# Gate and up products of three feed-forwards: the high weights meet both halves of the activations in one 512-column matmul

## The reference

```python
def swiglu(h, w_gate_up, w_down):
    gu = jnp.einsum("bsd,df->bsf", h, w_gate_up)
    g, u = jnp.split(gu, 2, axis=-1)
    return jnp.einsum("bsf,fd->bsd", jax.nn.silu(g) * u, w_down)

x = x + rmsnorm(swiglu(rmsnorm(x, g_pre), w_gate_up, w_down), g_post)        # first block
x = x + 0.5 * swiglu_2(rms_norm(x, norm_ffn1), ffn1_w1, ffn1_w3, ffn1_w2)    # second block, start
x = x + 0.5 * swiglu_2(rms_norm(x, norm_ffn2), ffn2_w1, ffn2_w3, ffn2_w2)    # second block, end
```

## Time and profile before

| | |
|---|---|
| median of 3 runs | 1049.44 us (1048.48 to 1049.68) |
| profiled execution, first to last instruction (span) | 1046.5 us |
| mean granted TensorE clock | 0.994 |
| TensorE matmul / weight load busy | 1022.3 / 1007.0 us |
| VectorE / ScalarE / GpSimd busy | 651.0 / 493.6 / 115.3 us |
| matmul records | 8282 |

### The profile page before, as it was taken

One profiled execution on the slowest core, in us unless ns is written; L12 is line 12 of the kernel. 1 busy time (PEld: TensorE's weight loads), 2 busy tenths in 40 slices (PEclk: granted clock), 3 DMA queues, 4 the chain that ended last, 5 costly groups with the idle time before them and its releaser, 6 DMA issues.

```text
span 1046.5 us, 19409 instructions
## 1 busy us (share of the span) xinstructions
PE 1022.3 (98%) x8282; PEld 1007.0 (96%) x8282; DVE 651.0 (62%) x616; ACT 493.6 (47%) x625; POOL 115.3 (11%) x91
## 2 busy tenths in 40 slices
PE   8999999998999999989999999999999999999997
PEld 7998999998999999979999999999999999999996
DVE  6655767958655555595555557775684475555554
ACT  5443445645433434554343434655755564343433
POOL 5000000566000000450000002000030020000000
PEclk9999999999999999999999999999999999999999
DMA  8653364453545565545646464633444345555531
GB/s 277 206 163 120 121 242 162 134 188 122 200 162 200 164 198 168 182 137 198 197 164 200 160 200 162 200 123 122 162 161 147 116 161 168 194 171 190 183 138 41
DMA packets 138107, 175.39 MB, mean 168 GB/s; under 512 B 3940, under 2 KB 122950, under 8 KB 137926
## 3 DMA queue, kind: packets, MB, share of 16 engines
q1 hardware_dynamic: 136006, 171.24, 49.7%
q10 hardware_dynamic: 2048, 3.38, 0.9%
HBM read 173.56 MB, written 1.05 MB: 167 GB/s over the span
## 4 chain that ended last, share of the span: by engine, by line
PE 88%; DVE 7%; issue 2%; ACT 1%; POOL 1%; DMA 1%; SPq 0%; DVEq 0%; ACTq 0%; POOLq 0%
PE bank L373 27%; PE bank L374 27%; PE bank L375 27%; DVE act_lo L1437 3%; DVE w_lo L1424 1%; PE bank L457 1%; DVE x_T L1539 1%; PE bank L821 1%; PE bank L842 1%; DMA stage<-in_w_in 1%; ACT w_hi L899 1%; PE bank L460 0%; PE bank L600 0%; DVE w_lo L1561 0%; PE bank L616 0%
## 5 line engine op out<-in xcount | busy, mean ns | idle before, releaser
L373 PE MATMUL bank<-act_hi,w_hi 128*128 128x256 f32 x1648 | 471.8, 286 | 12.7 <-DVE act_lo L1437 9.2
L374 PE MATMUL bank<-act_lo,w_hi 128*128 128x256 f32 x1648 | 467.5, 284 | 0.0
L375 PE MATMUL bank<-act_hi,w_lo 128*128 128x256 f32 x1648 | 467.4, 284 | 0.0
L373 PEld LDWEIGHTS bank<-act_hi,w_hi 128*128 128x128 f32 x1648 | 317.3, 193 | 18.1 <-DVE act_lo L1437 7.6
L374 PEld LDWEIGHTS bank<-act_lo,w_hi 128*128 128x128 f32 x1648 | 317.6, 193 | 0.1
L375 PEld LDWEIGHTS bank<-act_hi,w_lo 128*128 128x128 f32 x1648 | 317.4, 193 | 0.0
L1430 DVE TENSOR_TENSOR w_lo<-stage,w_hi 128x2048 fp32r<-128x2048 f32 x81 | 185.6, 2292 | 141.3 <-ACT w_hi L906 141.3
L1424 DVE TENSOR_TENSOR w_lo<-stage,w_hi 128x2048 fp32r<-128x2048 f32 x79 | 183.9, 2333 | 90.1 <-ACT w_hi L899 89.7
L899 ACT ACTIVATE w_hi<-stage 128x2048 fp32r<-128x2048 f32 x79 | 150.7, 1910 | 72.9 <-PE bank L375 71.0
L906 ACT ACTIVATE w_hi<-stage 128x2048 fp32r<-128x2048 f32 x81 | 154.0, 1902 | 54.8 <-PE bank L375 54.8
L373 PE MATMUL bank<-ffn_hi,w_hi 128*128 128x256 f32 x480 | 135.9, 283 | 0.0
(11 more groups left out here) (300 smaller groups left out, 1233.9 us busy)
## 6 DMA issues: line engine op xcount, KB each, us to landing
stage<-in_ffn_w SPq DMA_DIRECT2D x66, 1024.0 KB, 5.1
stage<-in_w_in SPq DMA_DIRECT2D x33, 1024.0 KB, 5.2
stage<-in_w_gate_up SPq DMA_DIRECT2D x22, 1024.0 KB, 5.1
stage<-in_w_down SPq DMA_DIRECT2D x11, 1024.0 KB, 4.8
stage<-in_w_out SPq DMA_DIRECT2D x8, 1024.0 KB, 4.9
stage<-in_mem_w_kv SPq DMA_DIRECT2D x8, 1024.0 KB, 5.3
stage<-in_w_branch SPq DMA_DIRECT2D x4, 1024.0 KB, 5.4
stage<-in_mem_w_q SPq DMA_DIRECT2D x4, 1024.0 KB, 4.9
```

Source lines behind the costliest of these rows:

```text
L373: pe.matmul(dst, w, x, start=first, stop=False, skip_group_check=not group)
L374: pe.matmul(dst, w, lo_x, start=False, stop=False, skip_group_check=not group)
L375: return pe.matmul(dst, lo_w, x, start=False, stop=last, skip_group_check=not group)
```

## The change

`act_hi` and `act_lo` become the two halves of one tile, so that for each k the 256 columns of the high part and the 256 of the low part are neighbours. In gate and up chunks, a step loads the high weights once and streams all 512 columns into a whole bank (first half high·high, second half high·low); the low weights' matmul of 256 columns adds to the second half. A chunk so takes two banks (one for each m): gate chunks have banks 2 and 3, up chunks banks 0 and 1, and gate 1 no longer has a bank of its own kind. 32 matmuls a chunk instead of 48, the same number of columns.

VectorE reads a chunk with a reduction that adds the two halves, 1024 elements into 512. rs is applied in operations of their own: to g after its reduction, and to the silu result; the up sum is multiplied with that. The square sum ahead of a feed-forward goes to bank ACC. Gate chunks wait for `gate_read`, up chunks for `up_read`. Outside the gate and up chunks of the feed-forwards no matmul changes.

```diff
-        act_hi = sb("act_hi", [P, KD, T], F32R)
-        act_lo = sb("act_lo", [P, KD, T], F32R)
+        act_both = sb("act_both", [P, KD, 2, T], F32R)
+        act_hi, act_lo = act_both[:, :, 0, :], act_both[:, :, 1, :]
...
+        up_banks, gate_banks = (ctx.enter_context(nc.psum_tensor(n, [P, 2, 512], F32)) for n in ("up_banks", "gate_banks"))
+        bank = [x[:, i, :] for x in (up_banks, gate_banks) for i in range(2)]
...
+        gate_halves, up_halves = (x[:, :, :].rearrange("p m (s t) -> p m t s", s=2) for x in (gate_banks, up_banks))
...
+            def halves_product(banks, place, ready=None, base=0):
...
+                def step(m, k):
+                    ms = slice(m * P, m * P + P)
+                    pe.matmul(banks[:, m, :], wh[:, k, ms], act_both[:, k, :, :].rearrange("p s t -> p (s t)"),
+                              start=k == 0, stop=False, skip_group_check=True)
+                    return pe.matmul(banks[:, m, T:2 * T], wl[:, k, ms], act_both[:, k, 0, :],
+                                     start=False, stop=k == KD - 1, skip_group_check=True)
...
+            def feed_forward(f, prep, norm, banks_before, extra=None):
+                base, n = FFN[f], f * PAIRS
+                pe.wait_ge(lo_done, base + 1)
+                aux(A_BEFORE_FFN[f])
+                pe.wait_ge(std_done, norm)
+                halves_product(gate_banks, base % RING, act_lo_done, 8 * prep)
+                sums(norm, ACC)
+                pe.wait_ge(lo_done, base + 2)
+                for c in banks_before:
+                    wait_read(pe, c)
+                halves_product(up_banks, (base + 1) % RING)
...
                 def body(t, first):
                     c = base + 2 + t * 3
                     pe.wait_ge(lo_done, c + 1)
+                    pe.wait_ge(gate_read, t + (n + 1))
+                    halves_product(gate_banks, s[0])
                     if first:
-
-                        aux(A_BEFORE_FFN[f])
-                    else:
-                        pe.wait_ge(up_free, t * 2 + (free + 1))
-                    up_product(pair[AUX if first else UP], s[0], act_hi, act_lo)
+                        pe.wait_ge(std_done, norm + 1)
...
                     ffn_chunk(c + 1, f, t, first, s[1])
                     pe.wait_ge(lo_done, c + 3)
-                    pe.wait_ge(up_free, t * 2 + (free + 2))
-                    up_product(pair[UP + 1], s[2], act_hi, act_lo)
+                    pe.wait_ge(up_read, t + (n + 1))
+                    halves_product(up_banks, s[2])
...
-                def gate_part(t, i, src=pair[UP]):
+                def gate_part(t, i):
+                    n = f * PAIRS + i + 1
                     dve.wait_ge(used, t * 3 + (base + (2 + 3 * (i - 1) if i else 0) + 1))
-                    dve.tensor_tensor(g_s, src, over(rs), ALU.mult).then_inc(up_free, 1)
+                    dve.tensor_reduce(g_s, gate_halves, AX, ALU.add).then_inc(gate_read, 1)
+                    dve.wait_ge(gate_read, t + n)
+                    dve.tensor_tensor(g_s, g_s, over(rs), ALU.mult).then_inc(gate_scaled, 1)
+
+                def silu_part(t, i):
+                    dve.wait_ge(silu_done, t + (f * PAIRS + i + 1))
+                    dve.tensor_tensor(silu, silu, over(rs), ALU.mult).then_inc(silu_scaled, 1)
...
-                    dve.tensor_tensor(u_s, pair[UP + 1], over(rs), ALU.mult).then_inc(up_free, 1)
-                    dve.wait_ge(up_free, t * 2 + (u0 + 2 * i + 2))
-                    dve.wait_ge(silu_done, t + n)
+                    dve.tensor_reduce(u_s, up_halves, AX, ALU.add).then_inc(up_read, 1)
+                    dve.wait_ge(up_read, t + n)
+                    dve.wait_ge(silu_scaled, t + n)
                     dve.tensor_tensor(h_T, u_s, silu, ALU.mult).then_inc(h_done, 1)
...
+                with dve.Fori(0, PAIRS - 2) as t:
                     lo_in_loop(t, base + 4)
-                    gate_part(t, 1, src)
+                    gate_part(t, 1)
                     lo_in_loop(t, base + 5)
+                    silu_part(t, 1)
                     lo_in_loop(t, base + 6)
                     up_part(t, 1, base + 4)
```

More of the change, by code:

```diff
@@ L40 @@
 FFN_CHUNKS = 3 * PAIRS
[L43 to L51, removed]
+BANK, BEFORE, FREED, AFTER_FFN = {}, {}, {}, {}
 BY_ACT = {V, V + 1, *range(OUT1, OUT1 + 4), *range(MEMK, MEMK + 4), *MEMV, DQ, DQ + 1, RV, RV + 1, DV, DV + 1,
@@ L71 @@
 through_banks(range(MEMQ, MEMQ + 4))
-through_banks(ffn_ups(FFN[2]))
-UP_FFN = [FREED[b] - 1 for b in FFN]
+AFTER_FFN[MEMV[0]] = AFTER_FFN[MEMV[1]] = 0
+AFTER_FFN[MEMV[3]] = AFTER_FFN[DQ] = 1
 def made(n):
@@ L426, in sums @@
                     pe.wait_ge(std_done, n)
-                pe.matmul(bank[SUM][:, 0:T], ones, sq_acc[:, 0, :], start=True, stop=True).then_inc(sum_done, 1)
+                pe.matmul(bank[to][:, 0:T], ones, sq_acc[:, 0, :], start=True, stop=True).then_inc(sum_done, 1)
             def sums_by_token(n):
@@ L487, in ffn_chunk @@
                      k_done if f == 0 and first == "first" else None)
[L489 to L493, removed]
+            def halves_product(banks, place, ready=None, base=0):
+                wh = w_hi[:, place, :].rearrange("p (k n) -> p k n", k=KD)
+                wl = w_lo[:, place, :].rearrange("p (k n) -> p k n", k=KD)
+                def step(m, k):
[4 more added lines that the diff above has]
+                                     start=False, stop=k == KD - 1, skip_group_check=True)
+                if ready is None:
+                    for m in range(2):
+                        for k in range(KD):
+                            mm = step(m, k)
+                else:
+                    for k in range(KD):
+                        pe.wait_ge(ready, base + k + 1)
+                        for m in range(2):
+                            mm = step(m, k)
+                mm.then_inc(used, 1)
+            def feed_forward(f, prep, norm, banks_before, extra=None):
[9 more added lines that the diff above has]
+                halves_product(up_banks, (base + 1) % RING)
                 s = [(base + 2 + j) % RING for j in range(3)]
@@ L1161, in _ @@
             hi(34)
-            deviation(3)
+            deviation(3, ACC)
             warm(ACT.Silu)
@@ L1183, in _ @@
             hi(70)
-            deviation(5)
+            deviation(5, ACC)
             warm(ACT.Silu)
@@ L1384, in _ @@
             hi(130)
-            deviation(8)
+            deviation(8, ACC)
             warm(ACT.Silu)
```

49 lines of the change are left out of this document (27 added, 22 removed).

## The result

| | before | after |
|---|---|---|
| median of 7 runs | 1049.74 us | 1052.95 us |
| ratio | | 1.0031 (95% interval 1.0020 to 1.0042) |
| span of the profiled execution | 1046.5 us | 1050.3 us |
| matmul records | 8282 | 7226 |

The change makes the kernel 0.31% slower, and the interval leaves no room for a gain. The forecast was 1038 us, faster. The profile before is of the fastest of its seven executions (1048.48 us), the one after of an execution 0.84 us under its median, so the spans differ by 3.8 us and the medians by 3.2.

A forecast was written before the change was run, and what follows sets the result against it. TensorE alone was taken to bound the feed-forwards. Savings of 4.45 us in the second and third and 3.0 in the first took 11.9 off 1046.5; with 2.94 for the median, 1037.5, say 1038 us; range 1033 to 1060.

The forecast's parts named there:

- the period: Three chunks (gate, up, down) inside a feed-forward on TensorE; forecast to go from 17.28 to 16.51 us.
- VectorE's longer ring: VectorE's in-order round with ScalarE, one up read to the next; forecast to grow from 13.82 to 16.30 us.
- TensorE, gate and up chunks: Gate and up matmuls: wide one 216 ns, narrow one 120, a step 336; each chunk 0.38 us less.
- rival B: Gate and up chunks: 13.3 ns stay with each matmul, wide one 226.6 ns; total 1046 us; chance 0.22.
- handovers: From the last down chunk of the first or second feed-forward to the next one's first up chunk; forecast change 0.
- rival C: Gate and up chunks: cost is by the column, wide matmul 237.3 ns; total 1054.5 us, slower; chance 0.12.
- Rival D: VectorE's two reductions: the split read is slow, 2.29 us each, VectorE becomes the bound; total 1100 us; chance 0.22.
- Start: Each feed-forward's start: gate 1 must wait for gate 0's reduction; 2.1 us later in the first, 1.07 in the others.
- End: Last chunks of a feed-forward: VectorE has less time, so the last down chunk waits; 0.62 us net loss each.
- D10: Last of a feed-forward's down chunks, numbered 0 to 10; forecast to start 17.9 us after the end of up 9.
- G10 and U10: Last gate and up chunks of a feed-forward, numbered 0 to 10; forecast to gain 0.77 us together.
- the prediction's own sums: Per feed-forward: start wait, less the saving of 16 chunks (15 in the first), plus 0.6 us at the end.

The follow-up runs named there:

- the uniform runs: A kernel of nothing but matmuls, 48 of one form back to back, each with its own weight load; in fp32r 120.0 ns for 256 columns, 227.5 for 512.
- the first run with GpSimd: Changed kernel with wide and narrow matmuls grouped, gate 0 read early, a low part moved, and silu's product with rs on GpSimd; 1045.02 us, ratio 0.9945.

## Why the prediction was wrong

*What bounds the kernel: right.* TensorE's stream sets the body, with or without the change; the period was filled in both, and VectorE's longer ring (16.13 us by its own steps, 16.30 forecast) stayed under it.

*TensorE, gate and up chunks: wrong, and this decided.* "I read the 120 as a load and a stream of nearly equal length in each other's way, take 216 for the wide matmul." The analogy was with plain fp32 matmuls, which have 2.7 ns beside their columns. fp32r matmuls with 128x128 weights have 13 to 14 ns each at any length from 256 to 512 columns (120.0 and 227.5 ns), which was rival B, and a load of 108 ns instead of 190 leaves the 120 at 118.3. On top of it came 5.6 ns for each pair that changes length, which no rival had. So a step took 353 ns for the 336 of the sum, and a chunk lost 0.105 us instead of 0.384: over the 53 chunks counted that is 14.8 us less gain. The whole error is 15 as well, partly by luck, since the other errors below nearly cancel (starts +0.9 us, handovers +1.4, ends -2.9). The time is also close to the 1054.5 us of rival C (a cost by the column), whose 237 ns resemble the 235 of a wide matmul in turns; the uniform runs rule its mechanism out. By the Trainium skill's formula that the prediction weighed ("TensorE: Matmul & The Clock Gate", Back-to-back issue gap; the page gives it for an isolated matmul) 216 and 109 make 325 a pair: bf16 matmuls took 216 and 109 in uniform runs and 325 in turns, fp32r ones 353.

*VectorE: right.* 1.22 us a reduction. The note on cachelines in the Trainium skill's "SBUF — State Buffer" speaks of matmuls where it comes to PSUM; the prediction carried it over to VectorE's reads, so that every element would pay for a new line. The reductions, which jump 1 KB between elements, don't bear that out. Rival D is gone.

*Start: right in kind, a little short.* +2.55 for 2.1 and +1.30 for 1.07. Alone in the kernel before, the bank costs 4.8 us and VectorE's longer work 5.7 in all, its part at the end and at the handovers included.

*End: too dear.* D10 starts 6.20 us after D9, 0.44 more than before, where 1.4 more was forecast. G10 and U10 gained 0.21 us instead of 0.77, which takes 0.56 off the wait. The rest is VectorE's chain: with T the end of U9 (626.56 us in the second feed-forward, two chunks of 5.653 ahead of D9), D10 started at T + 17.51 and not at T + 17.9.

*What was left out.* The handovers, +0.42 and +1.01. The prediction costed the wait at D10, not what VectorE does behind it, though it was the engine without idle time there. With the measured chunk, the prediction's own sums give (1.4 - 16 x 0.105 + 0.6) twice and 2.3 - 15 x 0.105 + 0.6: +2.0, or 1051.4 us; the handovers make it 1052.8. Measured: 1052.95. That is closer than the terms deserve. The lines of the table without the first add up to +2.5 us, since the end was cheaper than its 0.6, and the medians differ by 3.2. The 0.7 between them is not placed; the stretches of lower clock behind gate 1's wait are a candidate, and no run tests them alone.

What stays open: why an fp32r matmul has these 13 ns and pays for a change of length, and why wide matmuls in later groups take 230 ns and not 227.5, in the kernel (349 ns a pair) as in the run of nothing but matmuls (348.8). Open is also why the handovers kept their 0.4 and 1.0 us when the product on silu had left VectorE, and whether the wait at gate 1 brings the lower clock.

## What to carry to other kernels

Measure the pace of the very form of matmul before an edit that trades instructions for columns: joining two matmuls saves only the cost beside the columns, here 12.5 ns of 240, and nearly half of it went to the change of length. Weigh it against what the bank layout and the other engine pay where the pipeline fills and empties; that part is as long at each start and end however short the steady work gets. And follow the engine that becomes longer past the last wait, into the next stage: where it has no idle time, its delay shows up there.

## What the runs showed of the hardware

fp32r: 120.0, 146.7, 173.5 and 227.5 ns for 256, 320, 384 and 512 columns, and 5.6 ns more for a pair of 512 and 256 in turns than for the two apart; bf16 109 ns for 256 columns, 216 for 512 and 325 for such a pair. fp32r weight loads whose records take 108 ns (32 output columns) instead of 192 leave the pace of 256 columns within 2 ns. A VectorE reduction whose two inputs lie 1 KB apart in PSUM costs what neighbouring elements in SBUF cost, 1.22 us for 1024. A GpSimd product of 512 elements took 1.38 us on average. None of VectorE's products ran beside one, so no run shows what that costs; the two low parts and two reductions that did (from 470.07 and 857.88 us in the first run with GpSimd) took 2.29 and 1.22 us as elsewhere.
